# The weights' low part subtracted on POOL in pieces of 512 columns, with the steps of all engines merged in another order

## The reference, cut to what matters

```python
# block one, each of 2 layers
h = rms_norm(x, norm_gain);  proj = h @ w_in          # 1024 x 9304 weights
y_a = dsa_attention(q, k, v, q_idx, k_idx, w_idx) * silu(z_a)      # top 64 keys of each query
q, k, v = silu(causal_depthwise_conv(qkv_b, conv_w))
y_b = rms_norm(chunked_gated_delta_rule(l2(q), l2(k), v, beta, g)) * silu(z_b)
x = x + (gate0 * y_a + gate1 * y_b) @ w_out
x = rms_norm(x, final_gain)                            # after both layers
# block two, each of 2 layers
h = x @ w_in_2                                         # 1024 x 3620 weights
four branches: latent attention, stick-breaking, forgetting attention, attention to a memory
merged = sum(sigmoid(r @ w_merge_up)[n] * ((y_n * silu(gate_n)) @ w_branch[n]))
x = layer_norm(sqrt(2) * x + merged @ w_out_2)
```

## Time and profile before

| | us |
|---|---|
| median of 3 runs (1166.55 to 1167.27) | 1166.76 |
| the profiled execution | 1166.46 |
| its span, first to last instruction | 1164.6 |
| PE busy | 1078.2 (93%) |
| POOL busy | 662.5 (57%) |
| DVE busy | 646.9 (56%) |
| ACT busy | 584.2 (50%) |
| mean granted TensorE clock | 0.979 of 2.4 GHz |

### The profile page before, as it was taken

The page is one execution under the profiler, slowest core; times in us unless marked ns, Lnnn a source line. Parts: engine busy times, 40 slices in busy tenths (PEclk is TensorE's granted clock), DMA queues, the critical chain, the costliest instruction groups (busy, mean ns, idle before and its releaser), DMA issues.

```text
span 1164.6 us, 16977 instructions
## 1 busy us (share of the span) xinstructions
PE 1078.2 (93%) x6482; PEld 943.2 (81%) x6482; DVE 646.9 (56%) x1193; ACT 584.2 (50%) x859; POOL 662.5 (57%) x288
## 2 busy tenths in 40 slices
PE   5999999999979999999999999899998949999983
PEld 4988899888868998989888887688887738887773
DVE  3765463894665446546695475426645341845543
ACT  3643336454644463336656444354685434458542
POOL 3865345763527875446675355686456728644672
PEclk9999999999989999999999999999999969999997
DMA  8544233553234655233554233554324516523340
GB/s 286 168 142 131 90 109 109 163 146 91 91 126 120 185 156 159 73 109 111 148 160 131 75 109 119 178 162 139 109 91 147 176 56 213 142 87 118 114 148 37
DMA packets 84431, 152.07 MB, mean 131 GB/s; under 512 B 10560, under 2 KB 16512, under 8 KB 84352
## 3 DMA queue, kind: packets, MB, share of 16 engines
q1 hardware_dynamic: 84352, 151.00, 43.4%
HBM read 149.93 MB, written 1.05 MB: 130 GB/s over the span
## 4 chain that ended last, share of the span: by engine, by line
PE 82%; DVE 8%; ACT 5%; issue 2%; POOL 1%; DMA 1%; DVEq 0%; SPq 0%; ACTq 0%; POOLq 0%
PE bulk L825 46%; PE bulk L813 12%; PE chain L902 10%; PE chain L846 5%; ACT arena L1197 2%; PE bulk L818 1%; PE chain L1161 1%; POOL w_lo L767 1%; ACT w_hi L1197 1%; PE chain L884 1%; PE chain L1011 1%; PE chain L1027 1%; DVE arena L1592 1%; PE chain L1142 1%; ACT L1196 1%
## 5 line engine op out<-in xcount | busy, mean ns | idle before, releaser
L767 POOL TENSOR_TENSOR w_lo<-raw,w_hi 128x1024 fp32r<-128x1024 f32 (+3 forms) x284 | 662.3, 2345 | 479.6 <-ACT w_hi L1197 479.1
L1197 ACT ACTIVATE w_hi<-raw 128x1024 fp32r<-128x1024 f32 (+3 forms) x284 | 285.4, 1017 | 236.7 <-PE bulk L825 205.5
L825 PE MATMUL bulk<-w_hi,hT_hi 128*128 128x512 f32 (+1 forms) x768 | 312.1, 406 | 13.0 <-DVE arena L1674 6.6
L825 PE MATMUL bulk<-w_hi,hT_lo 128*128 128x512 f32 (+1 forms) x768 | 300.3, 391 | 0.0
L825 PE MATMUL bulk<-w_lo,hT_hi 128*128 128x512 f32 (+1 forms) x768 | 300.0, 391 | 0.0
L825 PEld LDWEIGHTS bulk<-w_hi,hT_hi 128*128 128x128 f32 x768 | 145.6, 190 | 46.2 <-DVE arena L1674 8.8
L825 PEld LDWEIGHTS bulk<-w_hi,hT_lo 128*128 128x128 f32 x768 | 145.1, 189 | 30.4
L825 PEld LDWEIGHTS bulk<-w_lo,hT_hi 128*128 128x128 f32 x768 | 145.5, 189 | 27.1 <-issue 1.2
L902 PE MATMUL chain<-arena 128*128 128x128 f32 x1056 | 133.5, 277 | 7.1 <-ACT arena L1197 4.3
L902 PEld LDWEIGHTS chain<-arena 128*128 128x128 f32 x1056 | 127.0, 191 | 15.3 <-ACT arena L1197 3.5
L813 PE MATMUL bulk<-hT_hi,w_hi 128*128 128x256 f32 x384 | 110.5, 288 | 0.0
(11 more groups left out here) (231 smaller groups left out, 1302.2 us busy)
## 6 DMA issues: line engine op xcount, KB each, us to landing
raw<-in_w_in_dram SPq DMA_DIRECT2D x194, 512.0 KB, 3.6
raw<-in_w_out_dram SPq DMA_DIRECT2D x32, 512.0 KB, 4.3
raw<-in_w_branch_dram SPq DMA_DIRECT2D x16, 512.0 KB, 3.9
raw<-in_w_mem_kv_dram SPq DMA_DIRECT2D x8, 512.0 KB, 3.7
raw<-in_w_merge_up_dram SPq DMA_DIRECT2D x16, 256.0 KB, 2.8
raw<-in_w_in_dram SPq DMA_DIRECT2D x8, 420.0 KB, 3.3
gain<-in_ln_rows_dram SPq DMA_DIRECT2D x4, 512.0 KB, 5.5
gain<-in_gains_dram SPq DMA_DIRECT2D x3, 512.0 KB, 6.5
```

The costliest lines, as they stand in the source:

```text
L767: pool.tensor_tensor(lo_of(p, u)[:, 0:n], raw_of(p, u)[:, 0:n], hi_of(p, u)[:, 0:n].bitcast(F32), ALU.subtract).then_inc(p.done("split"), 1)
L825: m = pe.matmul(dst, a, b[:, k, :], start=(kk == 0 and i == 0), stop=(kk == tot - 1 and i == 2))
L1197: return act.activation(dst, src, func, **more)
```

## The change

POOL's handler issues one subtraction for each 512 columns, and only the last one signals. The 252 units of 1024 columns get two instructions of 512, units of 840, 768 and 576 columns get 512 and the rest, units of 512 and 384 stay at one. What is waited for and what is signalled are the same. The string `ORDER` is another one with the same letters in the same numbers. Lanes, steps, slots and all other handlers stay.

```diff
-                    pool.tensor_tensor(lo_of(p, u)[:, 0:n], raw_of(p, u)[:, 0:n],
-                                       hi_of(p, u)[:, 0:n].bitcast(F32), ALU.subtract).then_inc(p.done("split"), 1)
+                    for a in range(0, n, 512):
+                        part = slice(a, min(a + 512, n))
+                        ins = pool.tensor_tensor(lo_of(p, u)[:, part], raw_of(p, u)[:, part],
+                                                 hi_of(p, u)[:, part].bitcast(F32), ALU.subtract)
+                    ins.then_inc(p.done("split"), 1)
```

```diff
 ORDER = (
-    "aaasaaammvsaasmsmasasaaaamascmcssmcammasmmcscsmsccsamcascmcmsscmaaasadsmasaamasamvmmaamsbbmssaaamsba"
...
-    "svssmsdysvmsmmssysvmssvsmmeemmem"
+    "aaaaaamsmsssvaamsamaasssaaammacmsmmmmascscmccmccsssasasmcacsmascadcaamsvsmamsaamasambsssdmcssmsaammb"
...
+    "sydsmmvsssvsmvmmyssssmvmvmeememm"
 )
```

More of the change, by code:

```diff
@@ L288 @@
-    "ssbsbmmdadbssbmamvaabmbbsssambdmsbambmdysbssadmsbmbambsdmbyysmsbamdsyavymbsymddysvmymmsvvdvsmsmmdmvm"
-    "svssmsdysvmsmmssysvmssvsmmeemmem"
+    "aaaaaamsmsssvaamsamaasssaaammacmsmmmmascscmccmccsssasasmcacsmascadcaamsvsmamsaamasambsssdmcssmsaammb"
+    "mmaaaamasdasamasmmaaasasamaadmasaasbasamabmaacmcsamcasmbbsaabacscmcmcmssbbbmasmscacmascsbcmaxassmaam"
+    "aamamsdsssbammaammsbbbmbsaaambsbxamdsasmscdasssdsmmwbsaabmsambbamabmsaamabmbssbbwbdssbmaamsaadmswaaw"
+    "maamamwssabxmamadbmssxasdmxaxasmxxswxxbbmsxmxssssvasvaaamammsmmmssmamasvmsmadmssamaasmmscsssmaccmasm"
@@ new lines @@
+    "mmmcscasccamsmcsacamcmassaasmdcmassaamcavasmmammsabsmsdasamsasaamaaasmsaasabsbmaaaasasmammaaamaddsam"
+    "aambmsascbmbssacabmsccmsabmcmsmcsxcbmsbmascaabcmmsbcasaasamasmcacadssammbmssamdmbmasasxbmasbbsbmbsss"
+    "sabadmmbabmaamwabmsdaasamabmwsmbsbabsbaasmsxbdamaamdamsmsasamwsmwbsasmaabmawsmdbmxamxsaadsswxxxsxxsb"
+    "mmmxxmsvmmvsmamsmmssssasmmdasaaassssssmsmmsmdsammmmmmdmsbssmdamssasambsmsmbaamasmbmsdabmbdasabbassms"
+    "dbsabbdmsmmaaasvbmsamsbmambsmbdbdsamsadyssbbmsmamydmbyabsydmsbysbmvymbsdmbbsvmbssmydsdydmmmvvsvsmmsy"
@@ L290 @@
+    "vdssvvmsmmmsmsysssmsvmmvsmsemmeeaamsssmsmmasdmsssmmsdmssmmsbmmdsabmassbammmsmsamaaadbssmsdbabsmbaabm"
+    "mabbsdbmsasdaasbmasmbmambssvsmdbbsdambmbdsmasbybmsabbmmbssdysmbadybmvsdsymdybssydmmsysvyvdmsmvmmmsmv"
+    "sydsmmvsssvsmvmmyssssmvmvmeememm"
 )
```

## The result

The changed kernel takes 1193.14 us in the median (1190.65 to 1196.48, 6 runs), the kernel before beside it 1167.01. The ratio is 1.0221, 95% interval 1.0196 to 1.0246: slower by 2.2%, where the forecast was 1163.3 us, in a range of 1155 to 1172. The profiled execution took 1190.68 us with a span of 1188.9, that is 24.3 us more than the span before. Lines behind the change have moved by three: L825 is L828 now, L2044 is L2047.

The account below looks back on a forecast made before the run. PE, busy for 93% of the span, was taken as the bound, with 39.5 us of idle time to win at most. Halves -1.8, the place traced +0.3 and other letters -2 gave -3.5: 1163.3 us, range 1155 to 1172.

Parts of the forecast that it names:

- Part 2: The new order of steps in `ORDER`: +0.3 us at one place traced, -2 us for the letters not priced singly.
- The bound of 6.5 us: How far merges differ: two layers of block two differ by 1.1 us of 190; six such stretches all one way, 6.5.
- The letters: Block one's delta-rule steps: counts of bulk units between them in the new order, read as more cover, supported taking -2 us.
- The place followed: Around `o(1,1)` and `memT(0)`: a 0.78 us wait goes, but `pT(1,1)` (1.09 us) moves behind `memT(0)`; together +0.3 us.
- The zero that it gave SP's queue: Layer norm rows of layer 0 no longer hold up nine unit loads; PE hardly waits for loads there, so 0.
- Part 1: Subtractions in halves: shorter DVE waits at three places, -4.1 us, PE's waits for POOL longer, +2.3; together -1.8.
- A: DVE doesn't get in between POOL's halves and waits out 2.58 instead of 2.40 us; 1166.7 us, no change; chance 0.15.
- B: `w_lo` comes late because each half can stand behind a DVE instruction, at eight units; 1172 us; chance 0.17.
- C: The new merge is worse by what merges differ, 6.5 us; 1172 us; chance 0.12.
- D: The new merge takes back a third of PE's 39.5 us of idle time; 1152 us; chance 0.12.

## Why the prediction was wrong

**The step that failed** is Part 2: "The rest of the 1132 letters I can't price one by one [...] I take -2, inside that and on the good side". The order alone, with the subtraction whole, costs a ratio of 1.0288, over 33 us; with the halves 1.0221 against 0.9991, 27 us. The bound of 6.5 us was four to five times too narrow. In its place the runs show new waits for DVE, ACT, issue and the memory (23 us with the subtraction whole) and 12.0 us more busy time. Two things were wrong in that bound. The two layers of block two are two samples of one list, made with the same care; they say how repeatable that list is, not how far another may be from it. And they were taken from the stretch that turned out least sensitive: 0.20% for both layers of block two, against 1.45% for layer 1 of block one and 0.69% for layer 0. Block one has the delta rule and the mixing, chains that block two has not; that these are why it is more sensitive is likely, not shown.

**The letters told nothing.** 57 instead of 47 steps with one unit between them, 2 instead of 10 with none, was read as more cover, but PE's waits for ACT went from 5.9 to 10.8 us. That "the units' subtractions also stand further ahead" was true of the list. Their distance is needed (31.4 us of waits without it), but PE waited for POOL 13 times instead of 6 all the same.

**The place followed** The earlier trace rows came out right as far as it was followed. The waits of 0.78 and 1.43 us went, the one for the memory became 6.76: 6.76 in place of 6.25 us. From the start of the 16 matmuls of `o(1,1)` to the transposes of `memT(0)` it is 9.58 us (337.63 to 347.21) instead of 9.46, with `pT(1,1)`, 1.03 us, now behind them; less the 0.78 that went ahead of them, this is 0.4 where the sum had +0.3. It was followed no further. The zero that it gave SP's queue was for the layer norm's rows; behind the memory's transfer a load came late for ACT, the squares stood behind that, and with `pT(1,1)` moved there too, `pv(1,1)` waited 2.33 us. The layer as a whole is 8.4 us longer.

**Part 1 fits as far as it can be told.** Forecast -1.8 us with ends -4.1 and +2.3; measured in the old order -1.0, with no change inside the interval. The gains are in the trace (2.17 and 2.30 us for the norm's two instructions, 2.19 for line 2047 at 713 instead of 3.27), and so are the costs: PE waited 8.6 us for POOL in 9 waits, 2.9 more than before, where 2.3 had been forecast. It left out that waits for ACT would grow by 1.5 us. It also counted nothing where small DVE steps follow each other; with two subtractions in a row that was too little, as the place at 441 us shows (PE stood 1.52 us instead of 2.65). In the reading of the wait list, "a microsecond or two each" passes over 11.3 us for the first norm, at the program's start, and the memory's 4.0; no sum rests on it.

**The rivals.** A, that the halves don't part, is false: DVE gets in between them, though no semaphore lies there. The page of the Trainium skill that spoke for it (GPSIMD Engine Reference, section 2.1 Instruction dispatch) says only how the engine's cores go from one instruction to the next; the trace shows that this doesn't keep DVE out. B, `w_lo` late, is there as a part: waits for POOL rose by 7.4 us in the changed kernel, by 2.9 with halves in the old order and by 0.4 with the new order alone. So it takes both; and in the new order the halves win more at DVE (14.6 us) than they lose here (7.0). C, the merge is worse, was the right case, with 6.5 where it was 27 to 33 us; it had a chance of 0.12 and a price that kept it at 1172. D, the merge takes back idle time, was false.

**Not in the prediction at all** was the clock. Of the 24.3 us, 9.8 are busy time. By the mean granted clocks, the changed kernel ran (1 - 0.970) x 2 x 1188.9 = 71 us at half the clock, the kernel before 49, and half of the 22 between them is 11 us, near the 9.8. The Trainium skill (TensorE: Matmul & The Clock Gate, section Terms) prices the loss by just that product, throttled time times the missing share of the clock; over the whole kernel the trace agrees. It does not hold stretch by stretch. In layer 0 of block one the granted clock fell too, 0.99 to 0.98 and 1.00 to 0.96, and PE's busy time didn't rise: the slow time fell into waits. Of the 20.5 us at half clock around the layer norm (0.58, 0.50 and 0.58 of the three windows above), most is a wait in which PE had no work, and filling it won 1.6 us and not 10. And with both waits filled, the changed kernel had nearly the mean clock of the kernel before and was not faster. So the clock is a part of the busy time; that it is a cause of the loss is not shown.

**What stays open.** The loss is located by stretch and by kind (idle time in many waits, and busy time, most of it at a lower clock), but the waits in layer 1 of block one were not each traced to the letters that make them. How much of the 9.8 us would come back if all idle stretches were filled wasn't shown: the two that were filled gave 2.7 and 0.5 us in the changed kernel, and 3.5 were lost behind the one for the memory. The two stretches at half clock in layer 1 of block one were not tried.

## What to carry to other kernels

When every engine walks one merged list, the order can be worth more than an edit whose mechanism is known, and counting letters did not price it; bound a new order by the idle time and the clock it may add, some per cent of the span, not by how alike two stretches of the old one are. Test the two parts of such a change apart first: here one pair of runs showed that the edit with the mechanism was worth 0.1% (0.7% in the new order, where there is more to wait for) and the one without was worth -2.9%. Before you take away a wait on the busiest engine, look at what follows it on the helper engines: their phase to each other was worth more than the wait where the product was moved ahead of the memory.

## What the runs showed of the hardware

- DVE gets at its data between two POOL instructions that follow each other without any semaphore between them. Over all DVE instructions, the longest stretch beyond the shortest of the same line and shape was 2.24 us in the kernel before, beside subtractions of 2.40 us, and 1.13 us in the changed kernel, beside subtractions of 1.29.
- In the places shown the hand-over goes in turn, one DVE instruction to one POOL instruction. So eight small DVE instructions beside four halves took 6.28 us instead of 2.19, and three instructions on a handful of numbers 1.2 us each instead of 0.17.
- Such a clash depends on phase: with POOL 1.6 us behind `mix_b` instead of 2.8, the same three DVE steps (`mix_b` and both of `mix`) took 11.0 instead of 6.7 us.
- The granted clock was 0.58 in the wait for the layer norm (13.7 us) and 0.50 in the work behind it. Filled with matmuls of the identity up to 1.44 us before the transposes, the wait had 1.00, and 16 transposes took 1.97 us; filled up to 3.67 us before them, they took 3.67.
- The clock also fell to half where PE had hardly stood: in 567.9 to 574.7 of the changed kernel, behind matmuls of one column and 1.3 us of idle time.
- A 128x128 matmul of float32 data by float32 data stands in the trace as two records of 0.113 us (160 records in 18.02).
